# An RWKV-7 core moved from 128x128 products to 64x64 tiles in the four quadrants of TensorE

## The reference

```python
def rwkv7_scan(r, w, k, v, a, b, s0):
    def step(S, inp):
        rt, wt, kt, vt, at, bt = inp
        sa = jnp.einsum('bhij,bhj->bhi', S, at)
        S = S * wt[:, :, None, :] + sa[..., None] * bt[:, :, None, :] + vt[..., None] * kt[:, :, None, :]
        return S, jnp.einsum('bhij,bhj->bhi', S, rt)
...
y, s = rwkv7_scan(rh, decay, kh, vh, -kk, kk * ah, wkv0)
y = head_group_norm(y, W['rw_lnx_g'][j], W['rw_lnx_b'][j])
y = y + jnp.sum(rh * kh * W['rw_r_k'][j], axis=-1, keepdims=True) * vh
out = (y.reshape(B, L, D) * g) @ W['rw_w_o'][j]
```

## Time and profile before

| | |
|---|---|
| median of three runs | 6027.74 us |
| span of the profiled execution | 6046.0 us |
| PE busy | 5438.2 us (90%) |
| PE weight loads busy | 4602.2 us (76%) |
| DVE busy | 2075.5 us (34%) |
| ACT busy | 992.5 us (16%) |
| instructions | 82156 |

### The profile page before, as it was taken

How to read it: one execution, slowest core, us unless ns; L and a number is a source line. 1 busy time by engine, 2 the same in 40 slices (tenths; PEclk the granted TensorE clock), 3 DMA queues, 4 the chain that set the end, 5 groups by cost and what they waited for, 6 DMA issues and landing times.

```text
span 6046.0 us, 82156 instructions
## 1 busy us (share of the span) xinstructions
PE 5438.2 (90%) x33415; PEld 4602.2 (76%) x33415; DVE 2075.5 (34%) x3008; ACT 992.5 (16%) x1207; POOL 262.7 (4%) x449
## 2 busy tenths in 40 slices
PE   7787878787999998899899999999999987999988
PEld 5566565676999996588778777777787777999977
DVE  2424242413333332400435435345354324333331
ACT  2212121102111112000111201201112003112121
POOL 1101111010000000200000000000000000000000
PEclk9989898988999999999979779788797798999999
DMA  2202121120111111121000000000000011111111
GB/s 60 70 26 63 34 54 42 30 67 21 43 46 43 43 38 32 31 75 68 25 17 15 3 15 3 17 15 3 17 15 3 1 37 32 43 46 43 43 35 51
DMA packets 305827, 206.22 MB, mean 34 GB/s; under 512 B 26664, under 2 KB 290782, under 8 KB 305438
## 3 DMA queue, kind: packets, MB, share of 16 engines
q1 hardware_dynamic: 290302, 161.38, 9.3%
q0 software_dynamic: 11584, 25.97, 1.6%
q10 hardware_dynamic: 3552, 13.41, 0.6%
HBM read 173.66 MB, written 27.04 MB: 33 GB/s over the span
## 4 chain that ended last, share of the span: by engine, by line
issue 40%; PE 34%; PEld 9%; DVE 6%; ACT 3%; POOLq 2%; DVEq 2%; PEldq 1%; ACTq 1%; POOL 1%; DMA 0%; SPq 0%
PE ps L1226 33%; PEld ps L1226 9%; DVE big L772 3%; ACT big L520 2%; POOLq L257 1%; DVE big L862 1%; DVEq L1151 1%; PE ps L1295 1%; POOLq L470 1%; ACT L520 0%; POOL big L259 0%; ACTq L612 0%; POOLq L259 0%; DVE big L919 0%; ACT xa L520 0%
## 5 line engine op out<-in xcount | busy, mean ns | idle before, releaser
L1226 PE MATMUL ps<-parts,wparts 128*128 128x272 f32 x12288 | 1558.8, 289 | 83.1 <-DVEq L993 83.1
L1226 PEld LDWEIGHTS ps<-parts,wparts 128*128 128x128 f32 x12288 | 1557.0, 190 | 84.7 <-DVEq L993 84.7
L1226 PE MATMUL ps<-big 128*128 128x128 f32 (+5 forms) x7960 | 1303.1, 319 | 179.8 <-ACTq L612 44.4
L1226 PEld LDWEIGHTS ps<-big 128*128 128x128 f32 (+2 forms) x7960 | 1070.7, 206 | 346.4 <-issue 80.9
L520 ACT ACTIVATE big<-ps 64x128 f32<-64x128 f32 (+6 forms) x434 | 252.4, 594 | 2964.8 <-PE ps L1226 1860.3
L1226 PE MATMUL ps<-xa,ring 128*128 128x272 f32 (+2 forms) x2496 | 681.2, 434 | 57.5 <-issue 43.6
L1226 PEld LDWEIGHTS ps<-xa,ring 128*128 128x128 f32 x2496 | 454.8, 192 | 283.8 <-issue 214.1
L1226 PE MATMUL ps<-big,ring 128*128 128x272 f32 (+4 forms) x2848 | 631.3, 383 | 35.0 <-DVEq L1053 20.1
L1226 PEld LDWEIGHTS ps<-big,ring 128*128 128x128 f32 (+3 forms) x2848 | 505.1, 181 | 160.5 <-issue 29.3
L772 DVE TENSOR_TENSOR big<-ps,big 128x512 f32<-128x512 f32 (+5 forms) x436 | 259.0, 603 | 555.6 <-PE ps L1226 299.3
L1226 PE MATMUL ps<-ident,ones 128*128 128x128 f32 x3072 | 431.0, 297 | 3.0 <-DVEq L861 3.0
(11 more groups left out here) (179 smaller groups left out, 3114.8 us busy)
## 6 DMA issues: line engine op xcount, KB each, us to landing
ring<-in_mlp_up SPq DMA_DIRECT2D x64, 512.0 KB, 4.0
ring<-in_mlp_down SPq DMA_DIRECT2D x64, 512.0 KB, 3.8
ring<-in_w_in_even SPq DMA_DIRECT2D x28, 512.0 KB, 7.0
rkv_scratch<-big ACTq DMA_DIRECT2D x24, 544.0 KB, 4.4
big<-rkv_scratch SPq DMA_DIRECT2D x24, 544.0 KB, 4.5
big<-in_cache_k SPq DMA_DIRECT2D x128, 64.0 KB, 1.9
big<-in_cache_k POOLq DMA_DIRECT2D x128, 64.0 KB, 2.2
big<-in_cache_v SPq DMA_DIRECT2D x128, 64.0 KB, 1.9
```

The lines of the kernel that those rows point to most:

```text
L1226: return pe.matmul(out, lhsT, rhs, start=start, stop=stop, skip_group_check=True)
```

## The change

The loops over pairs are unrolled. Prompt and sample tokens are separated: eight passes, each for a pair's 1024 prompt tokens, and a ninth for the 64 sample tokens of all pairs together (512 columns).

- Gram matrices, inverse, chain and outputs work on 64x64 tiles, one for each head h and chunk parity p. A tile lies on a half of the partitions that the code calls by h or p, and its result on another half; `TILES` goes through the four combinations, so that four consecutive products address the four quadrants of PE. Each product is again two pairs of a weight load and a matmul.
- One inverse serves both heads, in 5 levels after a first one made by DVE from a gram matrix. The running inverse is no longer summed by DVE: the identity is part of the operands, and ACT copies the products out of PSUM (128x1024). DVE only masks. There are no two groups.
- The chain keeps all 17 states (`SS`, 128x64 each, a head on each half); a chunk has two state products, one ACT copy, two B products and one DVE operation. The outputs are made after the chain, in bulk.
- No `warm` products are left in the core. At the end of a pass PE waits for DVE's last operation of it (`yo`).
- `xa` and most of `big` are used as work space. So the mixer's residual input goes to DRAM (`x1scr`, 4352 KB) before the core and comes back after it, and the core's output goes through `yscr`, from which `xa` is loaded (4352 KB) ahead of the output projection. Both loads stand on SyncE's queue ahead of the projection's weights.
- The LoRA weights are loaded once, not for each pair; the states of the samples are loaded by 32 DMAs near the end of the core, and stored by 32.

```diff
+TILES = ((0, 0), (1, 1), (0, 1), (1, 0))
...
+            def load_rkv(i):
+
+                if i:
+                    sp.wait_ge(a_mm, A_MM[i - 1, "tr3"])
+                    sp.wait_ge(a_dve, A_DVE[i - 1, "bon"])
                 for n, name in enumerate("RKV"):
...
+            sp.wait_ge(sg_ok, 1)
+            sp.dma_start(x1scr.rearrange("k p t -> p k t"), lo8.rearrange("p (k t) -> p k t", t=T)).then_inc(x1_st, 16)
...
+            sp.wait_ge(b_dve, B_DVE[KT, "yo"])
+            sp.wait_ge(yscr_st, 16 * (KT + 1))
+            sp.dma_start(xa[:, :].rearrange("p (k t) -> p k t", t=T), yscr.rearrange("k p t -> p k t")).then_inc(yscr_land, 16)
+            sp.wait_ge(wkv_stored, 16 * 40)
+            sp.dma_start(lo8.rearrange("p (k t) -> p k t", t=T), x1scr.rearrange("k p t -> p k t")).then_inc(x1_land, 16)
...
+            def a_inverse(i, nb, q):
...
+                for lv in range(1, levels):
+                    pb = 0 if lv % 2 else 2
+                    act.wait_ge(a_mm, A_MM[i, f"gx{lv}"])
+                    f(pair_of(w["C"], n), two(2 - pb, n), ACT.Copy).then_inc(a_act, 1)
+                    act.wait_ge(a_mm, A_MM[i, f"gxt{lv}"])
+                    f(pair_of(w["CI"], n), two(pb, n), ACT.Copy).then_inc(a_act, 1)
...
+                    act.wait_ge(b_mm, B_MM[i, f"u{c}"])
+                    f(half(w["US"], p, blk * P, P).rearrange("p (h v) -> p h v", h=2),
+                      two(4, CH)[p * 64:p * 64 + 64], ACT.Copy).then_inc(b_act, 1)
...
+                v.wait_ge(a_mm, A_MM[i, "gb"])
+                gram(mask, "AB", f"RB{q}", nb)
+                tt(c3(w["AB"]), c3(w["AB"]), one, ALU.add).then_inc(a_dve, 1)
...
+                    v.wait_ge(a_mm, A_MM[i, f"p1{lv}"])
+                    tt(w["EP"][:, 0:2 * n].rearrange("p (g b t) -> p g b t", g=2, t=CH),
+                       two(pb, n).rearrange("p g (b t) -> p g b t", t=CH),
+                       lm, ALU.mult).then_inc(a_dve, 1)
...
+                for c in range(NCH):
+                    v.wait_ge(b_mm, B_MM[i, f"s{c}"])
+                    v.scalar_tensor_tensor(out=w["SS"][:, (c + 1) * CH:(c + 2) * CH], in0=w["SS"][:, c * CH:(c + 1) * CH],
+                                           scalar=dec[:, q * NCH + c:q * NCH + c + 1], in1=bank(6 + c % 2, CH),
+                                           op0=ALU.mult, op1=ALU.add).then_inc(b_dve, 1)
...
+                def gram(keys):
+                    for blk in range(nb):
+                        for h, p in TILES:
+                            at = blk * P + p * CH
+                            rows = slice(h * 64, h * 64 + 64)
+                            out = ps[p * 64:p * 64 + 64, 2 * h * BANK + blk * P:2 * h * BANK + (blk + 1) * P]
+                            last = mm(out.rearrange("p (m t) -> p m t", m=2), half(w[keys], h, at), ar[rows, :, at:at + CH])
+                    return last
...
+                for lv in range(1, levels + 1):
+                    pb = 0 if lv % 2 else 2
+                    if lv > 1:
+                        pe.wait_ge(a_act, A_ACT[i, f"x{lv - 1}"])
+                    for blk in range(nb):
+                        for h, p in TILES:
+                            last = mm(out(pb + p, landing(lv, levels, h, p), blk), tile_(w["AB"], p, h, blk),
+                                      tile_(w["C"], p, x_of(h, p), blk))
+                    last.then_inc(a_mm, 1)
+                    pe.wait_ge(a_act, A_ACT[i, f"xt{lv - 1}"])
+                    pe.wait_ge(a_dve, A_DVE[i, f"p1m{lv}"])
+                    for blk in range(nb):
+                        for h, p in TILES:
+                            r = landing(lv, levels, h, p)
+                            xt, p1m = tile_(w["CI"], r, xt_of(h, p), blk), tile_(w["EP"], r, p, blk)
+                            if lv < levels:
+                                last = mm(out(2 - pb + r, p, blk), xt, p1m)
+                            else:
+                                last = mm(out(2 - pb + r, p, blk), p1m, xt)
+                    last.then_inc(a_mm, 1)
...
+                            last = mm(out(pb + r, landing(lv + 1, levels, h, p), blk), p1m, xt)
+                    last.then_inc(a_mm, 1)
...
                 for c in range(NCH):
...
+                    if c:
+                        pe.wait_ge(b_dve, B_DVE[i, f"st{c - 1}"])
+                        for h in range(2):
+                            last = mm(half(bank(4 + h), p, 0), half(tat, h, (p * BLKS + blk) * CH), half(w["SS"], h, c * CH),
+                                      False, True)
+                    last.then_inc(b_mm, 1)
...
+                    pe.wait_ge(b_act, B_ACT[i, f"u{c}"])
+                    for h in range(2):
+                        last = mm(half(bank(6 + p), h, 0), half(btk, p, blk * P + h * CH), half(us, p, blk * P + h * CH),
+                                  False, True)
...
+            for i in range(KT):
+                a_prep(i, BLKS, i % 2)
+                a_rows(i, BLKS, i % 2)
+                a_grams(i, BLKS, i % 2)
+                a_inverse(i, BLKS, i % 2)
+                b_chain(i, i % 2)
+                b_norm(i, U1)
+                pe.wait_ge(b_act, B_ACT[i, "rs"])
+                pe.wait_ge(b_dve, B_DVE[i, "yo"])
+            a_prep(KT, 4, 0)
```

More of the change, by code:

```diff
@@ L188, in trunk_program, with half, landing @@
+        def half(t, r, at, n=CH):
+            return t[r * 64:r * 64 + 64, at:at + n]
+        def landing(lv, levels, h, p):
+            return h ^ p if (levels - lv) % 2 == 0 else h
         w_land = [sem(f"w_land{s}") for s in range(SLOTS)]
@@ new lines, in trunk_program, with count_steps @@
+        a_mm, a_act, a_dve, b_mm, b_act, b_dve, ws_land = (sem(n) for n in (
+            "a_mm", "a_act", "a_dve", "b_mm", "b_act", "b_dve", "ws_land"))
+        prompt_pairs = range(KT)
+        def count_steps(prompt, sample):
+            value, n = {}, 0
+            for i in (*prompt_pairs, KT):
+                for name in (prompt if i < KT else sample).split():
+                    n += 1
+                    value[i, name] = n
+            return value
+        chain = lambda *names: " ".join(f"{n}{c}" for c in range(NCH) for n in names)
@@ L504, in _ @@
[L504 to L512 removed]
+            pool.drain()
@@ L1630, in y_part @@
-                def y_part(rows, m, r, blk, lo, stop):
-                    for h in range(2):
-                        out = pset(0, lo, 64, 64 * h, 64 * h + 64)
-                        tc = m * T + blk * P + r
-                        last = mm(out, rows[r:r + 64, blk * P + 64 * h:blk * P + 64 * h + 64],
-                                  w[f"RB{h}"][r:r + 64, tc:tc + 64], False, stop and h == 1)
+                        pe.wait_ge(a_dve, A_DVE[i, "bh"])
+                        pe.wait_ge(a_act, A_ACT[i, f"tr{n - 2}"])
@@ L1637, in y_part, with b_chain, u_rest @@
+            def b_chain(i, q):
+                xth, akv, tat = w[f"XTH{q}"], w[f"AKV{q}"], w[f"TAT{q}"]
+                btk, ktk, vtk, us = w[f"BTK{q}"], w[f"KTK{q}"], w[f"VTK{q}"], w["US"]
+                def u_rest(c):
+                    p, blk = c % 2, c // 2
+                    for h in range(2):
+                        last = mm(half(bank(4 + h), p, 0), half(xth, h, ((h ^ p) * BLKS + blk) * CH),
+                                  half(akv, h, (p * BLKS + blk) * CH), True, c == 0)
                     return last
@@ L1646, in _ @@
+                pe.wait_ge(a_act, A_ACT[i, "akv"])
+                pe.wait_ge(a_act, A_ACT[i, "tat"])
+                last = u_rest(0)
                 keys_values(0)
                 for c in range(NCH):
-                    r, blk = c % 2 * 64, c // 2
-                    st = state[:, c % 2 * P:(c % 2 + 1) * P]
-                    pe.wait_ge(st_ok, i * 17 + c + 1)
-                    mm(bank(3 + c % 2, P, 0, r, r + 64), w["TAT"][:, c * CH:(c + 1) * CH], st,
-                       False, True).then_inc(us_mm, 1)
@@ L1696, in _ @@
-            pe.wait_ge(rw_out, KT)
+                for turn in range(2):
+                    for blk in range(BLKS):
+                        for h in range(2):
+                            p = h ^ turn
+                            c = 2 * blk + p
+                            last = mm(half(bank(4 + p), h, blk * CH), half(w["SS"], h, c * CH),
+                                      half(w[f"ARR{q}"], h, c * CH), blk == 0, False)
+                    last.then_inc(b_mm, 1)
+                    pe.wait_ge(b_mm, B_MM[i, f"yi{turn}"])
@@ new lines, in _ @@
+            pe.wait_ge(a_act, A_ACT[KT, "akv"])
+            pe.wait_ge(a_act, A_ACT[KT, "tat"])
+            for i in range(KT):
+                p, blk = i % 2, i // 2
+                for h in range(2):
+                    mm(half(bank(4 + h), h, i * CH), half(w["AKV0"], h, (p * 4 + blk) * CH),
+                       half(w["XTH0"], h, ((h ^ p) * 4 + blk) * CH), i == 0, False)
+                for b in range(NSEQ):
+                    for h in range(2):
```

(12 more changed lines are left out.)

935 lines of the change are left out of this document (514 added, 421 removed).

## The result

The changed kernel takes 5347.1 us (median of 4 runs, 5340.96 to 5350.0) against 6035.5 us for the one before (6021.8 to 6051.7): a ratio of 0.886, 95% interval 0.883 to 0.888. The profiled execution took 5344.39 us, with a span of 5342.7.

What follows compares the result with a forecast made beforehand. The chain was taken as bound by PE's throughput at half clock, the inverse by its 128x128 products. 8 x (167 - 242.4) + 125 + 2 + 35 gave -441 us, span 5605, time 5590 us; range 5380 to 5860.

Steps and rivals of the forecast that it cites:

- The ninth pass: Sample tokens of all pairs handled together after the eight prompt passes: 125 us (80 to 175), replacing 8 x 12.0 us.
- the tail: Core's end: last store, two 4352 KB loads and weights ahead of the output projection, 40 us unhidden, where PE waited some 5.
- the price of a small tile: 64x64 weight load plus 64-column matmul on PE: 36 ns a pair, so 2.3 us for a 64-pair step.
- Its own bound from below: Lowest price of a small pair: four quadrants side by side at full clock, 0.0535/4, 13 ns.
- quicker than that: Rival, chance 0.13: four quadrants near 20 ns a pair regain full clock; 133 us a pass, 110 for the ninth, 5320 us.
- The step's use: Inverse: five levels, each three serial steps of 64 pairs (6.9 us), mask 1.22 and hand-overs 0.6: 8.7 us each.
- The half clock as assumed: PE stays at half clock throughout the core, no fillers being left; 512-column products take 0.85 us instead of about 0.43.
- It costs little at 36 ns: Claim that half clock in the core costs little at this pair price, apart from the 512-column products.
- Issue-bound: Rival, chance 0.24: after each wait the sequencer issues pairs at 57 ns whatever quadrants could take; steps 3.6 us, 5840 us.
- No overlap: Rival, chance 0.05: quadrants do not overlap when every product is a new tile; 105 ns a pair, about 6550 us.
- Instructions: Rival, chance 0.06: supply of some 16000 unrolled pairs, wanted three times as fast, limits the core; about 5950 us.
- the hidden loads of r, k and v: Next pair's loads wait only for early readers and stay hidden: 4.4 us for 544 KB.

Runs made afterwards that it cites:

- the first experiment: Changed kernel with only the 64x64 product order altered in grams, inverse, AKV and TAT: one quadrant's eight products follow one another; 6072.5 us (one run).

## Why the prediction was wrong

Forecast and measured for a pass of the profiled execution, in us:

| | preparation | grams | inverse, AKV, TAT | chain | outputs | norm | sum |
|---|---|---|---|---|---|---|---|
| forecast | 37.3 | 19.9 | 53.2 | 29.9 | 9.3 | 17.5 | 167 |
| measured | 33.5 | 16.1 | 39.4 | 27.3 | 6.5 | 13.0 | 136 |

The table has the third pass. On the mean a pass takes 136.2 us, 30.8 less than forecast, which is 246 us for eight. The ninth pass (122.9 against 125) gives 2, the tail (30.8 against 40) 9, and the start of the first pass some 4: 2 us more were forecast for its LoRA weights, and PE waited 11.28 us for them where the kernel before had waited 13.75. That makes up the 262 us between a span of 5605 and 5342.7.

**The step that failed is the price of a small tile, 36 ns a pair, where it measured 15 (full clock) to 27 (half).** The prediction read three quadrants at work together at the half clock in the earlier trace rows and took three for the count; but a step of the changed kernel has four, so that the same 0.105 us round gives 26 ns even there, and it set the half clock for the whole core on the ground of the earlier trace rows. Its own bound from below, 13 ns, held, and so did the mechanism of the rival "quicker than that": PE worked 26.0 us in the inverse for 1152 pairs (22.6 ns each, 41.5 us forecast), 7.0 us in the grams (9.1) and 5.3 in the outputs (8.0). That is 20 us a pass, the three stages together are shorter by as much, and over eight passes it makes 162 of the 262. Of the 13 ns between 36 and 22.6, the count of quadrants is 9 (36 to 27, both at the half clock) and the clock 4. One quadrant in turn shows that the low price hangs on the order of the tiles: with it the whole gain, 688 us, is gone.

**The step's use was right.** With 27 ns at full clock a level took 6.71 us at best and 7.03 on the mean, with its three steps in a row; 192 x 9 ns more make 8.4 to 8.8 us at 36 ns, an estimate from these two, where 8.7 were forecast.

**The half clock as assumed** cost a part of the rest. The norm measured a clock of 1.00, its head sums 1.98 us and not 3.4, and the stage was 4.5 us shorter: 36 us over eight passes. Eight transposes took 1.05 us and not 1.7. The chain's 2.6 us a pass are not the clock's, which stood at 0.54 there. "It costs little at 36 ns" did not hold at lower prices: right-sized fillers give 47 us.

**The rival "quicker than that"** had a chance of 0.13 and was right in its marks, though in part only: steps of 1.1 us where the clock was full (of the 40 first steps of a level 29 stood at 1.00 and 9 at 0.50), ACT's copy as releaser ahead of 15 of these 40, 133 us a pass (136 measured), 5320 us (5347). That it came within 27 us owes something to luck, for it had full clock, no idle times and 110 us for the ninth pass, where 122.9 were measured. The Trainium skill's "TensorEngine Tiling (Array Packing)", section "PSUM Bottleneck", has it that the copies out of PSUM may become the bottleneck behind a fourfold speedup. The trace agrees in part: the first step of a level waits 0.20 us for the copy at full clock, and a level of 4.89 us without idle times has the copy in its chain. What spoke for this rival, four quadrants and a density like that of the inverse before, deserved more than 0.13. The range stopped 33 us above the result because it counted this rival in only in part.

**Issue-bound** is out: 15 ns a pair is far under the 57 of the earlier trace rows. The Trainium skill's "TensorE: Matmul & The Clock Gate", section "Wait — 56ns, not 53.3ns?", gives about 62 ns for each matmul without hardware decoding; no row shows which decoding is at work here, and nothing like 62 ns binds. The same section has it that the time from start to start never drops below about 25 ns with either; the trace disagrees for products that alternate between quadrants, with 15 ns a pair. **No overlap** is out as a fact of the kernel after, and is real as a fact of the order: the first experiment measured 89 ns and a time 40 us above the kernel before, near the 72 ns at which the prediction saw the gain gone. **Instructions**: the supply may show, as 31 us of idle times and not as a new bound. That these are waits for instructions is inferred, not shown: from their spacing (256 instructions or a multiple), from their having no releaser and from their absence with one quadrant in turn and all but one with two, with the same instructions. What was fetched when, no row shows.

**Right were** the tail's mechanism (two transfers ahead of the projection; 9 us too dear, since the two loads landed 24.6 us behind the first one's issue and not 32.4), the ninth pass to 2 us as a sum, the chain (27.3 against 29.9: a chunk 1.71 us and not 1.87, bound by hand-overs as forecast), and the hidden loads of r, k and v.

## To carry over

Count how many quadrants of the array consecutive small products address, for the price of a 64x64 tile falls with that number (89 ns a pair with one at the half clock, 27 with two and 15 with four at full), and an order of loops can be worth the whole change. Once the tiles are cheap, the engine that was the bound is idle for 44% of the core: then the next gain lies in other work beside the serial chain (-233 us here), not in still cheaper products. A cost read at one degree of concurrency and one clock has to be worked out for both before a range is set.

## What was not expected of the hardware

- PE can be busy all through a stretch and stand at the half clock: in the first experiment 10.70 us of 10.70 in one quadrant at a time, clock 0.50; with two quadrants in turn it was busy 79% of the inverse at 0.90, with four 66% at 0.78.
- Pairs of a 64x64 fp32 weight load and product start 15 ns apart on average over four quadrants in turn at full clock (58 ns a round of four), and 27 ns at the half clock (107 ns a round). Whether two quadrants share rows, columns or neither made no difference (27 to 28 ns).
- Idle times of 0.2 to 2.1 us inside unrolled steps, 128 pairs (256 instructions) apart or a multiple, 30 of them in the changed kernel; none with one quadrant in turn, and one of 0.30 us with two.
- Work in bulk can pay for itself through the clock: without the output products ahead of them the norm's head sums took 3.48 to 3.78 us instead of 1.98.
